# A decoder trunk kernel: another order of the steps where one sub-layer hands over to the next, and products sorted by kind

## Chip, cores and metric

One core of a Trainium2 chip runs the whole program in one launch. The metric is the device time of one execution in microseconds (us), median of several runs.

## What is computed

One decoder layer on 544 tokens (512 of a prompt, 8 x 4 of samples), width 1024:

```
rms(x, g) = x * rsqrt(mean(x*x) + 1e-6) * g
x = x + 0.5 * rms(ffn(rms(x, ffn1_pre_g)), ffn1_post_g)      # ffn(h) = (silu(h Wg) * (h Wu)) Wd, width 2816
x = x + rms(mix(rms(x, mix_pre_g)), mix_post_g)              # mix: one input projection (2432 columns), four
x = x + 0.5 * rms(ffn(rms(x, ffn2_pre_g)), ffn2_post_g)      # token mixers of width 256, one output projection
```

The mixers are a gated conv of width 3, a conv of width 31 with LayerNorm, RWKV-7 time mixing in four heads, and pooled means; their states are returned too. All is float32.

## The kernel before

The activations lie transposed: x is 8 rows (k or j, 128 features each) of 544 tokens; the tokens are halved into half 0 and half 1 of 272, since a PSUM bank takes 512 numbers. A *unit* is one tile of 128 output features. A weight tile comes by DMA into `raw` (2 slots, SP's queue), ScalarE copies it to `wh` (fp32r, `split_hi`, L284), VectorE takes the rest to `wl` (`split_lo`, L289); both have 4 slots. The input is split in the same way (`xh`, `xl`, or `hh`, `hl`). `product` forms for each row j and each half the three products wh x right_h, wh x right_l and wl x right_h (L305 to L307), accumulated in one bank per half. Unit s writes banks 2s and 2s+1 (`pair(s)`). Every engine has its own order written out by hand; semaphores join them, and VectorE and ScalarE take their steps strictly as written.

The program is FFN 1, a hand-over (n = 1), the mixer, a hand-over (n = 3), FFN 2, and an end (n = 5). In a hand-over the norm behind a sub-layer (gain g_n) and the one ahead of the next (g_n+1) are taken together:

- `last_units_pe`: of the last 8 output units, units 4 to 7 are made first for half 0, then for half 1 (`second`). VectorE takes each half out of PSUM (`leave_half`, L896 or L1967), forms its product with x (`half_cross_dve`, L472), ScalarE the squares (L466, L468), and VectorE adds the three sums of squares into `a3` (`half_squares_dve`, L488; of unit 7 in two steps, L491 and L494; of whole units `squares_dve`, L447).
- `half_sums_pe(n, h, second)` (L367) sums a3 over the partitions: first the squares of f, then (second) those of f*g and f*g*x, out of which the sum of squares of the new x follows, so that the next norm's root is known before x is. `var_dve` (L401), `half_root_act` (L386, L389; second L383), `half_rec_dve` (L409) and for the second `square_dve` (L418 to L426) make the factors, `half_spread_pe` (L376) spreads one over the partitions, `half_rb_act` (L393) copies it to SBUF.
- `rows_dve`: for each row k, update (L511: f*g*factor), add to x (L516), and `low` (L526, xl); ScalarE's `high_act` (L521) makes xh from the new x between add and low.
- `ramp_pe`: the first four units of the next sub-layer, made row by row as the rows come, half 0, then half 1. Unit 3 of half 0 joins at row 4 with five rows at once. At the end of half 1 the units finish one after the other.

Each of sums and spreads needs what VectorE has added; VectorE's `var_dve` and `square_dve` need the sums; `update` needs the copied factor; the row needs xl. Behind the ramp, VectorE takes the first unit out of PSUM (L1831 in the mixer) and the next unit's weight tile is split.

Of the kernel before, what the change touches and what calls it, by code (L numbers as in the profile page):

```python
# [32 lines left out]
KD = D // P  # L33
# [3 lines left out]
H = N // 2  # L37
# [77 lines left out]
def program(nc, a, o):  # L115

    with ExitStack() as ctx:
# [180 lines left out]
        def product(pe, out, s, order, right_h, right_l, before=None, opens=True, closes=True, parts=(0, 1)):  # L298

            for j in order:  # L300
                if before:
                    before(j)
                for n in parts:
                    col = slice(n * H, n * H + H)
                    pe.matmul(out[:, n], wh[:, s, j], right_h[:, j, col], start=opens and j == order[0], stop=False)  # L305
                    pe.matmul(out[:, n], wh[:, s, j], right_l[:, j, col], start=False, stop=False)  # L306
                    last = pe.matmul(out[:, n], wl[:, s, j], right_h[:, j, col], start=False, stop=closes and j == order[-1])  # L307
            return last


# [218 lines left out]
        def rows_dve(dve, n, h, first, last):  # L529

            for k in range(first, last):
                update_dve(dve, n, h, k)
                if k:
                    low_dve(dve, n, h, k - 1)
                add_dve(dve, n, h, k)
            if last == KD:
                low_dve(dve, n, h, KD - 1)

        def last_units_pe(pe, n, u0, first, order, right_h, right_l, free):

            for d in range(4, KD):
                split_ready(pe, u0, 0, first + d)
                free(d)
                product(pe, pair(d - 4), d - 4, order, right_h, right_l, parts=(0,)).then_inc(S("half_done"), 1)

            def second(d, lo, hi):
                return product(pe, pair(d - 4), d - 4, order[lo:hi], right_h, right_l, opens=lo == 0, closes=hi == KD, parts=(1,))

            second(4, 0, 5)
            half_sums_pe(pe, n, 0, 0)  # L550
            second(4, 5, 8).then_inc(S("unit_done"), 1)
            if n < 5:
                half_sums_pe(pe, n, 0, 1)
            second(5, 0, 2)
            half_spread_pe(pe, n, 0, 0)
            second(5, 2, 8).then_inc(S("unit_done"), 1)
            second(6, 0, 8).then_inc(S("unit_done"), 1)
            if n < 5:
                half_spread_pe(pe, n, 0, 1)
            second(7, 0, 8).then_inc(S("unit_done"), 1)  # L560

        def ramp_pe(pe, n, u):

            def come(h, j):
                pe.wait_ge(S("n_xl"), row(n, h, j) + 1)

            pe.wait_ge(S("n_rb"), mark(n, 0, 1) + 1)
            for j in range(KD):
                come(0, j)
                for s in range(3):  # L570
                    if j == 0:
                        split_ready(pe, u, 0, s)
                    product(pe, pair(s), s, (j,), xh, xl, opens=j == 0, closes=j == KD - 1, parts=(0,))
                if j == 2:
                    half_sums_pe(pe, n, 1, 0)
                if j == 3:
                    half_sums_pe(pe, n, 1, 1)
                    half_spread_pe(pe, n, 1, 0)
                if j == 4:
                    split_ready(pe, u, 0, 3)  # L580
                    product(pe, pair(3), 3, range(5), xh, xl, closes=False, parts=(0,))
                if j > 4:
                    product(pe, pair(3), 3, (j,), xh, xl, opens=False, closes=j == KD - 1, parts=(0,))
                if j == 5:
                    half_spread_pe(pe, n, 1, 1)
            pe.wait_ge(S("n_rb"), mark(n, 1, 1) + 1)
            for j in range(KD - 2):
                come(1, j)
                for s in range(4):
                    product(pe, pair(s), s, (j,), xh, xl, opens=j == 0, closes=False, parts=(1,))  # L590
            for s in range(4):
                product(pe, pair(s), s, (KD - 2, KD - 1), xh, xl, None if s else lambda j: come(1, j), opens=False, parts=(1,)
                        ).then_inc(S("unit_done"), 1)

        def hand_over_act(act, n, u):
            for d in range(4, KD):
                half_squares_act(act, n, 0, d)
            half_root_act(act, n, 0, 0)
            split_hi(act, u, 0, 0, KD)
            half_squares_act(act, n, 1, 4)  # L600
            half_rb_act(act, n, 0, 0)
            high_act(act, n, 0, 0)
            split_hi(act, u, 0, 1, KD)
            half_root_act(act, n, 0, 1)
            high_act(act, n, 0, 1)
            half_squares_act(act, n, 1, 5)
            split_hi(act, u, 0, 2, KD)
            half_rb_act(act, n, 0, 1)
            high_act(act, n, 0, 2)
            half_squares_act(act, n, 1, 6)  # L610
            high_act(act, n, 0, 3)
            split_hi(act, u, 0, 3, KD)
            half_squares_act(act, n, 1, 7)
            half_root_act(act, n, 1, 0)
            high_act(act, n, 0, 4)
            high_act(act, n, 0, 5)
            half_rb_act(act, n, 1, 0)
            high_act(act, n, 0, 6)
            half_root_act(act, n, 1, 1)
            high_act(act, n, 0, 7)  # L620
            high_act(act, n, 1, 0)
            half_rb_act(act, n, 1, 1)
            for k in range(1, KD):
                high_act(act, n, 1, k)

        def hand_over_dve(dve, n, u, leave_half):
            for d in range(4, KD):
                leave_half(0, d)
                half_cross_dve(dve, n, 0, d)
                half_squares_dve(dve, n, 0, d)  # L630
            var_dve(dve, n, 0)
            half_rec_dve(dve, n, 0, 0)
            leave_half(1, 4)
            half_cross_dve(dve, n, 1, 4)
            split_lo(dve, u, 0, 0, KD)
            half_squares_dve(dve, n, 1, 4)
            rows_dve(dve, n, 0, 0, 1)
            square_dve(dve, n, 0)
            rows_dve(dve, n, 0, 1, 2)
            leave_half(1, 5)  # L640
            half_cross_dve(dve, n, 1, 5)
            half_rec_dve(dve, n, 0, 1)
            split_lo(dve, u, 0, 1, KD)
            rows_dve(dve, n, 0, 2, 3)
            half_squares_dve(dve, n, 1, 5)
            split_lo(dve, u, 0, 2, KD)
            leave_half(1, 6)
            half_cross_dve(dve, n, 1, 6)
            rows_dve(dve, n, 0, 3, 4)
            leave_half(1, 7)  # L650
            half_cross_dve(dve, n, 1, 7)
            half_squares_dve(dve, n, 1, 6)
            half_squares_dve(dve, n, 1, 7)
            var_dve(dve, n, 1)
            rows_dve(dve, n, 0, 4, 5)
            half_rec_dve(dve, n, 1, 0)
            split_lo(dve, u, 0, 3, KD)
            rows_dve(dve, n, 0, 5, 6)
            square_dve(dve, n, 1)
            rows_dve(dve, n, 0, 6, 7)  # L660
            half_rec_dve(dve, n, 1, 1)
            rows_dve(dve, n, 0, 7, 8)
            rows_dve(dve, n, 1, 0, 8)

        BY_POOL = (0, 1, 3, 4, 6)

# [160 lines left out]
        def ffn_act(act, q, u0, n):  # L827
            u = u0
# [3 lines left out]
            for g, (f0, nf) in enumerate(GROUPS):  # L832
# [11 lines left out]
                            silu_act(act, q, i, f0, 1 + s // 2)  # L844
                u += 2 * nf
                for s in range(KD):
                    if g == 2 and s == 7:
                        down_act(act, q, g, 3, n)
                    split_hi(act, u, 0, s, nf)
                    if s == 1:  # L850
                        silu_act(act, q, 0, f0, nf - 1)
                        if g == 2:
                            act.activation(st2[:, 1, 6:7], ones[:, 0:1], ACT.Sqrt)
                    if g == 2 and 2 <= s < 5:
                        down_act(act, q, g, s - 2, n)
                u += KD

        def ffn_dve(dve, q, u0, n):
# [4 lines left out]
            for g, (f0, nf) in enumerate(GROUPS):  # L863
# [20 lines left out]
                    if g == 2 and s == 6:  # L884
                        down_dve(dve, q, u, g, 3, n)
                u += KD
            squares_dve(dve, n, 3)

            def leave_half(h, d):
                if h:  # L890
# [788 lines left out]
        def mixer_act(act):  # L1679
# [64 lines left out]
                act.wait_ge(S("c_y"), p + 1)  # L1744
                split_y_hi(act, 6 + p)
            for m in range(4):
                if m == 2:
                    split_hi(act, MIX0, 0, OUT0 + 4 + m, KD)
                act.wait_ge(S("o_out"), m + 1)
                squares_act(act, 3, m, f[:, m], par_("g3", m))  # L1750
                if m != 2:
                    split_hi(act, MIX0, 0, OUT0 + 4 + m, KD)

        def mixer_dve(dve):
# [194 lines left out]
            for m in range(4):  # L1949
# [7 lines left out]
                cross_dve(dve, 3, m)  # L1957
                if m != 2:
                    split_lo(dve, MIX0, 0, OUT0 + 4 + m, KD)
            squares_dve(dve, 3, 3)  # L1960

            def leave_half(h, d):
                if h:
# [161 lines left out]
```

## Time and profile before

| | |
|---|---|
| median of 3 runs | 1209.89 us (1205.71 to 1211.03) |
| the profiled execution | 1210.43 us, span of its instructions 1208.6 us |
| busy: TensorE, its weight loads | 1151.0 us (95%), 1128.4 us (93%) |
| busy: VectorE, ScalarE, GpSimd | 626.6 us (52%), 336.8 us (28%), 40.2 us (3%) |
| DMA | 92.23 MB, 76 GB/s over the span |
| first hand-over, second hand-over | about 396 to 457, 754 to 815 us of the span |

All times in the rows are us from the span's start. Busy times are shares of the span per engine and overlap each other. A matmul's record lasts longer than the distance to the next one, since matmuls are pipelined; the distance between two starts is what one costs.

### The profile page before, as it was taken

What the parts mean: (1) busy time and instruction counts of PE and PEld (TensorE: products, weight loads), DVE (VectorE), ACT (ScalarE), POOL (GpSimd) and SP (SyncE); (2) the same over time, 40 slices, a digit from 0 to 9 for tenths busy, and PEclk for the clock granted to TensorE, in tenths of its full rate; (3) what the DMA queues carried; (4) which work ended last, traced back from release to release, by engine and by line L of the source; (5) the groups of instructions that cost most, each with busy time, mean ns of one, the idle gap of its engine ahead of it and who ended that gap; (6) DMA issues with size and microseconds to landing.
All of it is one profiled execution on the core that took longest, in us unless ns stands there. A gap on an engine that the chain in (4) does not pass through costs nothing.

```text
span 1208.6 us, 21735 instructions
## 1 busy us (share of the span) xinstructions
PE 1151.0 (95%) x8994; PEld 1128.4 (93%) x8994; DVE 626.6 (52%) x1075; ACT 336.8 (28%) x496; POOL 40.2 (3%) x57
## 2 busy tenths in 40 slices
PE   6999999999999997999898989999999999999996
PEld 6999999999999997998777889899999999999996
DVE  5533343333345775889767526865333343334346
ACT  5321222112223433521234343433122221122220
POOL 0000000000000000210221100000000000000001
PEclk9999999999999888999899989889999999999998
DMA  6313232223232211332500002203233232323222
GB/s 229 105 53 104 89 102 71 88 87 103 71 102 78 65 50 53 76 88 76 41 10 28 1 1 73 70 18 105 69 106 102 72 103 72 105 70 101 72 70 75
DMA packets 35391, 92.23 MB, mean 76 GB/s; under 512 B 10368, under 2 KB 12928, under 8 KB 35200
## 3 DMA queue, kind: packets, MB, share of 16 engines
q1 hardware_dynamic: 33744, 87.67, 24.5%
q10 hardware_dynamic: 1584, 3.68, 0.8%
q8 instruction: 45, 0.74, 0.3%
q14 instruction: 18, 0.15, 0.0%
HBM read 88.05 MB, written 3.28 MB: 76 GB/s over the span
## 4 chain that ended last, share of the span: by engine, by line
PE 83%; DVE 11%; issue 3%; ACT 2%; DMA 1%; ACTq 0%; DVEq 0%; SPq 0%
PE ps L305 24%; PE ps L307 24%; PE ps L306 24%; PE ps L1131 1%; DVE wl L289 1%; PE ps L1137 1%; PE ps L1138 1%; PE ps L367 1%; DVE mixf L984 1%; ACT wh L284 1%; DVE a L447 1%; PE ps L376 1%; DVE tb L676 1%; PE ps L1573 1%; DVE xx L1310 0%
## 5 line engine op out<-in xcount | busy, mean ns | idle before, releaser
L305 PE MATMUL ps<-xh,wh 128*128 128x272 f32 x1840 | 543.1, 295 | 24.9 <-DVE xl L503 11.0
L307 PE MATMUL ps<-xh,wl 128*128 128x272 f32 x1840 | 538.5, 293 | 0.0
L306 PE MATMUL ps<-xl,wh 128*128 128x272 f32 x1840 | 535.9, 291 | 0.0
L305 PEld LDWEIGHTS ps<-xh,wh 128*128 128x128 f32 x1840 | 352.9, 192 | 27.4 <-DVE wl L289 17.4
L306 PEld LDWEIGHTS ps<-xl,wh 128*128 128x128 f32 x1840 | 353.6, 192 | 0.1
L307 PEld LDWEIGHTS ps<-xh,wl 128*128 128x128 f32 x1840 | 352.4, 192 | 0.0
L284 ACT ACTIVATE wh<-raw 128x1024 fp32r<-128x1024 f32 (+1 forms) x163 | 167.8, 1033 | 322.1 <-PE ps L307 199.4
L289 DVE TENSOR_TENSOR wl<-raw,wh 128x1024 fp32r<-128x1024 f32 (+1 forms) x163 | 192.5, 1202 | 46.3 <-ACT wh L284 46.0
L305 PE MATMUL ps<-hh,wh 128*128 128x272 f32 x704 | 204.1, 290 | 0.0
L307 PE MATMUL ps<-hh,wl 128*128 128x272 f32 x704 | 203.6, 289 | 0.0
L306 PE MATMUL ps<-hl,wh 128*128 128x272 f32 x704 | 203.0, 288 | 0.0
L797 DVE TENSOR_TENSOR h<-silu,ps 128x544 f32<-128x544 f32 x44 | 31.7, 721 | 212.6 <-PE ps L307 210.6
L306 PEld LDWEIGHTS ps<-hl,wh 128*128 128x128 f32 x704 | 133.4, 190 | 0.0
L305 PEld LDWEIGHTS ps<-hh,wh 128*128 128x128 f32 x704 | 133.2, 189 | 0.0
L307 PEld LDWEIGHTS ps<-hh,wl 128*128 128x128 f32 x704 | 133.1, 189 | 0.0
L783 ACT ACTIVATE silu<-silu 128x544 f32<-128x544 f32 x44 | 29.0, 659 | 233.9 <-DVE silu L793 233.9
L793 DVE TENSOR_TENSOR silu<-ps,rb 128x544 f32<-128x544 f32 x44 | 31.8, 724 | 80.2 <-PE ps L307 75.9
L816 DVE TENSOR_TENSOR f<-ps,f 128x544 f32<-128x544 f32 x24 | 17.4, 724 | 76.3 <-PE ps L307 76.3
L984 DVE SCALAR_TENSOR_TENSOR mixf<-zb,par,mixf 128x512 f32<-128x512 f32 x60 | 44.6, 743 | 0.1
L804 DVE TENSOR_TENSOR hl<-h,hh 128x544 f32 (+1 forms) x44 | 31.9, 725 | 4.3
L813 DVE COPY f<-ps 128x544 f32<-128x544 f32 x16 | 11.6, 724 | 43.2 <-PE ps L307 43.2
L1310 DVE TENSOR_TENSOR xx<-ps,con 128x256 f32<-128x256 f32 x40 | 16.7, 422 | 26.9 <-PE ps L1131 26.4
(311 smaller groups left out, 855.4 us busy)
## 6 DMA issues: line engine op xcount, KB each, us to landing
raw<-in_w_gu SPq DMA_DIRECT2D x88, 512.0 KB, 3.7
raw<-in_w_d SPq DMA_DIRECT2D x32, 512.0 KB, 3.7
raw<-in_w_in SPq DMA_DIRECT2D x19, 512.0 KB, 3.7
raw<-in_w_d SPq DMA_DIRECT2D x16, 384.0 KB, 3.1
raw<-in_w_out SPq DMA_DIRECT2D x8, 512.0 KB, 3.7
x<-in_x ACTq DMA_DIRECT2D x8, 272.0 KB, 6.8
out_y<-x SPq DMA_DIRECT2D x16, 136.0 KB, 1.8
con<-in_con ACTq DMA_DIRECT2D x1, 1158.5 KB, 9.3
```

Of the source, the lines that this page charges most:

```text
L284: act.activation(wh[:, s % 4, 0:k, :], raw[:, s % RAW, 0:k, :], ACT.Copy).then_inc(S("w_hi"), 1 + skip)
L289: dve.tensor_tensor(wl[:, s % 4, 0:k, :], raw[:, s % RAW, 0:k, :], wh[:, s % 4, 0:k, :].bitcast(F32), SUB).then_inc(S("w_lo"), 1 + skip)
L305: pe.matmul(out[:, n], wh[:, s, j], right_h[:, j, col], start=opens and j == order[0], stop=False)
L306: pe.matmul(out[:, n], wh[:, s, j], right_l[:, j, col], start=False, stop=False)
L307: last = pe.matmul(out[:, n], wl[:, s, j], right_h[:, j, col], start=False, stop=closes and j == order[-1])
L783: act.activation(silu[:, s % 2], silu[:, s % 2], ACT.Silu).then_inc(S(f"silu{q}"), 1)
L793: dve.tensor_tensor(halves(silu[:, s % 2]), pair(2 * (s % 2)), halves(rb[:]), MUL).then_inc(S(f"gate{q}"), 1)
L797: dve.tensor_tensor(halves(h32[:, s % 2]), halves(silu[:, s % 2]), pair(2 * (s % 2) + 1), MUL).then_inc(S(f"h_mul{q}"), 1)
L804: dve.tensor_tensor(hl[:, j].rearrange(one), h32[:, s % 2], hh[:, j].rearrange(one).bitcast(F32), SUB).then_inc(S(f"h_lo{q}"), 1)
L816: dve.tensor_tensor(halves(f[:, d]), pair(d % 4), halves(f[:, d]), ADD).then_inc(S(f"d_out{q}"), 1)
L984: eng.scalar_tensor_tensor(y1, z1, w, y1, MUL, ADD)
L1310: dve.tensor_tensor(xx[:, p], done(p)[:, 0:2 * P].rearrange(HC, h=2), C_("lev", k=l * P).unsqueeze(1).to_broadcast([P, 2, P]), MUL).then_i ...
```

## The change

The order of steps changes, and no work is added or removed. In `product` the three kinds are the outer loop and the two halves the inner one. In the hand-overs: the last whole unit's squares (`squares_dve`, 3) and each half unit's squares are added a unit later; TensorE's first sums stand after six rows of unit 4 and the second root's sums go from there to unit 6 (half 0), and from row 3 to behind the loop (half 1); the first sums of half 1 go from row 2 to row 4; the spreads move with them; waits for `h_square` are added ahead of unit 1 in the ramp, where its bank held those sums; unit 3 joins at row 4 in both halves; ScalarE's and VectorE's orders are rewritten to fit; in a row, the add stands right behind the update. In two places a weight copy of ScalarE goes ahead of a whole unit's squares.

```diff
@@ -300,11 +300,11 @@
             before(j)
-        for n in parts:
-            col = slice(n * H, n * H + H)
-            pe.matmul(out[:, n], wh[:, s, j], right_h[:, j, col], start=opens and j == order[0], stop=False)
-            pe.matmul(out[:, n], wh[:, s, j], right_l[:, j, col], start=False, stop=False)
-            last = pe.matmul(out[:, n], wl[:, s, j], right_h[:, j, col], start=False, stop=closes and j == order[-1])
+        for left, right in ((wh, right_h), (wh, right_l), (wl, right_h)):
+            first, final = left is wh and right is right_h, left is wl
+            for n in parts:
+                last = pe.matmul(out[:, n], left[:, s, j], right[:, j, n * H:n * H + H], start=first and opens and j == order[0],
+                                 stop=final and closes and j == order[-1])
     return last
@@ -530,9 +530,9 @@
         update_dve(dve, n, h, k)
+        add_dve(dve, n, h, k)
         if k:
             low_dve(dve, n, h, k - 1)
-        add_dve(dve, n, h, k)
     if last == KD:
@@ -546,17 +546,16 @@
     def second(d, lo, hi):
...
-    second(4, 0, 5)
+    second(4, 0, 6)
     half_sums_pe(pe, n, 0, 0)
-    second(4, 5, 8).then_inc(S("unit_done"), 1)
+    second(4, 6, 8).then_inc(S("unit_done"), 1)
+    second(5, 0, 3)
+    half_spread_pe(pe, n, 0, 0)
+    second(5, 3, 8).then_inc(S("unit_done"), 1)
+    second(6, 0, 4)
     if n < 5:
         half_sums_pe(pe, n, 0, 1)
-    second(5, 0, 2)
-    half_spread_pe(pe, n, 0, 0)
-    second(5, 2, 8).then_inc(S("unit_done"), 1)
-    second(6, 0, 8).then_inc(S("unit_done"), 1)
-    if n < 5:
-        half_spread_pe(pe, n, 0, 1)
+    second(6, 4, 8).then_inc(S("unit_done"), 1)
     second(7, 0, 8).then_inc(S("unit_done"), 1)
...
 def ramp_pe(pe, n, u):
@@ -564,30 +563,41 @@
     def come(h, j):
...
-    pe.wait_ge(S("n_rb"), mark(n, 0, 1) + 1)
+    def fourth(h, j):
+        if j == 4:
+            split_ready(pe, u, 0, 3)
+            pe.wait_ge(S("n_rb"), mark(n, h, 1) + 1)
+            product(pe, pair(3), 3, range(5), xh, xl, closes=False, parts=(h,))
+        if j > 4:
+            product(pe, pair(3), 3, (j,), xh, xl, opens=False, closes=j == KD - 1, parts=(h,))
+
+    pe.wait_ge(S("n_rb"), mark(n, 0, 0) + 1)
     for j in range(KD):
...
                 split_ready(pe, u, 0, s)
+                if s == 1:
+                    pe.wait_ge(S("h_square"), 10 * (n // 2) + 2)
             product(pe, pair(s), s, (j,), xh, xl, opens=j == 0, closes=j == KD - 1, parts=(0,))
-        if j == 2:
+        if j == 1:
+            half_spread_pe(pe, n, 0, 1)
+        fourth(0, j)
+        if j == 4:
             half_sums_pe(pe, n, 1, 0)
-        if j == 3:
-            half_sums_pe(pe, n, 1, 1)
+        if j == 6:
             half_spread_pe(pe, n, 1, 0)
-        if j == 4:
-            split_ready(pe, u, 0, 3)
-            product(pe, pair(3), 3, range(5), xh, xl, closes=False, parts=(0,))
-        if j > 4:
-            product(pe, pair(3), 3, (j,), xh, xl, opens=False, closes=j == KD - 1, parts=(0,))
-        if j == 5:
-            half_spread_pe(pe, n, 1, 1)
-    pe.wait_ge(S("n_rb"), mark(n, 1, 1) + 1)
+    half_sums_pe(pe, n, 1, 1)
+    pe.wait_ge(S("n_rb"), mark(n, 1, 0) + 1)
     for j in range(KD - 2):
         come(1, j)
-        for s in range(4):
+        for s in range(3):
+            if j == 0 and s == 1:
+                pe.wait_ge(S("h_square"), 10 * (n // 2) + 5 + 2)
             product(pe, pair(s), s, (j,), xh, xl, opens=j == 0, closes=False, parts=(1,))
+        if j == 2:
+            half_spread_pe(pe, n, 1, 1)
+        fourth(1, j)
     for s in range(4):
@@ -597,70 +607,80 @@
     split_hi(act, u, 0, 0, KD)
+    half_rb_act(act, n, 0, 0)
     half_squares_act(act, n, 1, 4)
-    half_rb_act(act, n, 0, 0)
     high_act(act, n, 0, 0)
     split_hi(act, u, 0, 1, KD)
-    half_root_act(act, n, 0, 1)
     high_act(act, n, 0, 1)
...
     split_hi(act, u, 0, 2, KD)
-    half_rb_act(act, n, 0, 1)
     high_act(act, n, 0, 2)
+    half_root_act(act, n, 0, 1)
     half_squares_act(act, n, 1, 6)
...
     split_hi(act, u, 0, 3, KD)
+    half_rb_act(act, n, 0, 1)
     half_squares_act(act, n, 1, 7)
+    high_act(act, n, 0, 4)
     half_root_act(act, n, 1, 0)
-    high_act(act, n, 0, 4)
     high_act(act, n, 0, 5)
+    high_act(act, n, 0, 6)
+    high_act(act, n, 0, 7)
     half_rb_act(act, n, 1, 0)
-    high_act(act, n, 0, 6)
+    high_act(act, n, 1, 0)
     half_root_act(act, n, 1, 1)
-    high_act(act, n, 0, 7)
-    high_act(act, n, 1, 0)
+    for k in range(1, 4):
+        high_act(act, n, 1, k)
     half_rb_act(act, n, 1, 1)
-    for k in range(1, KD):
+    for k in range(4, KD):
         high_act(act, n, 1, k)
...
 def hand_over_dve(dve, n, u, leave_half):
     for d in range(4, KD):
+        if d == 7:
+            half_squares_dve(dve, n, 0, 6)
         leave_half(0, d)
         half_cross_dve(dve, n, 0, d)
-        half_squares_dve(dve, n, 0, d)
+        if d == 4:
+            squares_dve(dve, n, 3)
+        elif d < 7:
+            half_squares_dve(dve, n, 0, d - 1)
+    half_squares_dve(dve, n, 0, 7)
     var_dve(dve, n, 0)
...
     half_cross_dve(dve, n, 1, 4)
+    rows_dve(dve, n, 0, 0, 1)
     split_lo(dve, u, 0, 0, KD)
+    rows_dve(dve, n, 0, 1, 2)
     half_squares_dve(dve, n, 1, 4)
-    rows_dve(dve, n, 0, 0, 1)
-    square_dve(dve, n, 0)
-    rows_dve(dve, n, 0, 1, 2)
     leave_half(1, 5)
     half_cross_dve(dve, n, 1, 5)
-    half_rec_dve(dve, n, 0, 1)
     split_lo(dve, u, 0, 1, KD)
     rows_dve(dve, n, 0, 2, 3)
-    half_squares_dve(dve, n, 1, 5)
+    square_dve(dve, n, 0)
     split_lo(dve, u, 0, 2, KD)
...
     half_cross_dve(dve, n, 1, 6)
+    half_rec_dve(dve, n, 0, 1)
     rows_dve(dve, n, 0, 3, 4)
+    half_squares_dve(dve, n, 1, 5)
     leave_half(1, 7)
     half_cross_dve(dve, n, 1, 7)
+    rows_dve(dve, n, 0, 4, 5)
     half_squares_dve(dve, n, 1, 6)
+    split_lo(dve, u, 0, 3, KD)
     half_squares_dve(dve, n, 1, 7)
+    rows_dve(dve, n, 0, 5, 6)
     var_dve(dve, n, 1)
-    rows_dve(dve, n, 0, 4, 5)
+    rows_dve(dve, n, 0, 6, 7)
     half_rec_dve(dve, n, 1, 0)
-    split_lo(dve, u, 0, 3, KD)
-    rows_dve(dve, n, 0, 5, 6)
+    rows_dve(dve, n, 0, 7, 8)
+    rows_dve(dve, n, 1, 0, 1)
     square_dve(dve, n, 1)
-    rows_dve(dve, n, 0, 6, 7)
+    rows_dve(dve, n, 1, 1, 2)
     half_rec_dve(dve, n, 1, 1)
-    rows_dve(dve, n, 0, 7, 8)
-    rows_dve(dve, n, 1, 0, 8)
+    rows_dve(dve, n, 1, 2, 8)
@@ -844,9 +864,9 @@
         for s in range(KD):
+            split_hi(act, u, 0, s, nf)
             if g == 2 and s == 7:
                 down_act(act, q, g, 3, n)
-            split_hi(act, u, 0, s, nf)
             if s == 1:
@@ -884,7 +904,8 @@
         u += KD
-    squares_dve(dve, n, 3)
+    if n == 5:
+        squares_dve(dve, n, 3)
     def leave_half(h, d):
@@ -1744,11 +1765,11 @@
     for m in range(4):
-        if m == 2:
+        if m >= 2:
             split_hi(act, MIX0, 0, OUT0 + 4 + m, KD)
...
         squares_act(act, 3, m, f[:, m], par_("g3", m))
-        if m != 2:
+        if m < 2:
             split_hi(act, MIX0, 0, OUT0 + 4 + m, KD)
...
 def mixer_dve(dve):
@@ -1957,7 +1978,6 @@
             split_lo(dve, MIX0, 0, OUT0 + 4 + m, KD)
-    squares_dve(dve, 3, 3)
     def leave_half(h, d):
...
```

## Rows read from the trace of the kernel before

**Rows 1.** the page: the chain that ended last, shares of the span

```profile
PE 83%; DVE 11%; issue 3%; ACT 2%; DMA 1%; ACTq 0%; DVEq 0%; SPq 0%
```

**Rows 2.** stretches: busy us (x instructions) by engine, granted clock, DMA

```profile
130.00:220.00 90.00, 90.00 (x716) 90.00 (x715) 34.92 (x43) 20.30 (x23) 0.00 (x0) 1.00 0.28 88
230.00:260.00 30.00, 30.00 (x241) 30.00 (x241) 9.28 (x10) 5.31 (x5) 0.00 (x0) 1.00 0.30 88
425.70:429.00 3.30, 1.93 (x16) 1.62 (x14) 2.89 (x7) 1.41 (x4) 0.00 (x0) 1.00 0.01 2
429.10:439.30 10.20, 10.20 (x46) 10.20 (x47) 6.60 (x20) 2.67 (x6) 0.00 (x0) 0.50 0.40 139
787.50:797.60 10.10, 10.10 (x47) 10.10 (x48) 6.56 (x21) 2.67 (x6) 0.00 (x0) 0.50 0.15 54
```

**Rows 3.** VectorE in order of time, start and duration in us

```profile
395.06 1.23 DVE L289 TENSOR_TENSOR wl<-raw,wh 128x1024 fp32r<-128x1024 f32 x1 [1.70 <-ACT wh L284]
396.21 1.85 DVE L447 TENSOR_TENSOR a<-a,sq 128x1632 f32<-128x1632 f32 x1
397.98 0.43 DVE L896 TENSOR_TENSOR f<-ps,f 128x272 f32<-128x272 f32 x1
398.44 0.50 DVE L472 SCALAR_TENSOR_TENSOR sq<-f,par,x 128x272 f32<-128x272 f32 x1
399.37 1.01 DVE L488 TENSOR_TENSOR a<-a,sq 128x816 f32<-128x816 f32 x1 [0.43 <-ACT sq L468]
400.30 0.43 DVE L896 TENSOR_TENSOR f<-ps,f 128x272 f32<-128x272 f32 x1
...
405.95 0.44 DVE L491 TENSOR_TENSOR a<-a,sq 128x272 f32<-128x272 f32 x1
406.31 0.72 DVE L494 TENSOR_TENSOR a<-a,sq 128x544 f32<-128x544 f32 x1
```

**Rows 4.** TensorE's sums (L367) and spreads (L376), full or half clock

```profile
406.45 0.83 PE L367 MATMUL ps<-con,a 128*128 128x1 f32 x6 [1.81 <-DVE a L491]
...
408.36 2.34 PE L367 MATMUL ps<-con,a 128*128 128x1 f32 x12
...
412.06 1.29 PE L376 MATMUL ps<-con,st 128*128 128x128 f32 x6
...
441.47 0.74 PE L376 MATMUL ps<-con,st 128*128 128x128 f32 x6
```

**Rows 5.** ScalarE's copies of the spread factors

```profile
413.39 0.40 ACT L393 ACTIVATE rbp<-ps 128x272 f32<-128x272 f32 x1 [2.71 <-PE ps L376]
...
442.24 0.40 ACT L393 ACTIVATE rb<-ps 128x272 f32<-128x272 f32 x1 [1.71 <-PE ps L376]
```

**Rows 6.** VectorE: rows as before, and what stands between them

```profile
413.82 0.50 DVE L511 SCALAR_TENSOR_TENSOR tb<-f,par,rbp 128x272 f32<-128x272 f32 x1 [1.69 <-ACT rbp L393]
414.36 0.44 DVE L516 TENSOR_TENSOR x<-x,tb 128x272 f32<-128x272 f32 x1
414.72 0.15 DVE L418 SCALAR_TENSOR_TENSOR st<-ps,st 128x3 f32<-128x3 f32 x1
...
415.57 0.49 DVE L511 SCALAR_TENSOR_TENSOR tb<-f,par,rbp 128x272 f32<-128x272 f32 x1
415.98 0.49 DVE L526 SCALAR_TENSOR_TENSOR xl<-x,par,xh 128x272 fp32r<-128x272 f32 x1
416.39 0.43 DVE L516 TENSOR_TENSOR x<-x,tb 128x272 f32<-128x272 f32 x1
```

**Rows 7.** groups by line: the weight loads of two neighbours with one weight

```profile
L306 PEld LDWEIGHTS ps<-xl,wh 128*128 128x128 f32 x1840 | 353.6, 192 | 0.1
L305 PEld LDWEIGHTS ps<-xh,wh 128*128 128x128 f32 x1840 | 352.9, 192 | 27.4 <-DVE wl L289 17.4 <-issue 4.5 <-DVE xl L1554 3.2
```

**Rows 8.** VectorE: the wait after a ramp, and the last half

```profile
455.20 1.61 DVE L1831 TENSOR_TENSOR pc<-ps,rb 128x272 f32<-128x272 f32 x6 [2.66 <-PE ps L307]
...
1196.22 0.43 DVE L896 TENSOR_TENSOR f<-ps,f 128x272 f32<-128x272 f32 x1
```

## The prediction

> **What bounds the kernel now.** I read the page's chain first. TensorE holds 83% of it, VectorE 11% [rows 1], so a saving must shorten TensorE's stream or take waits out of it. Then the stretches: in plain products TensorE is busy throughout, one 272-column product per about 126 ns (714 whole ones in 90.00 us; 239 in 30.00 us with hh as the right side, 125.5 ns) [rows 2]. 272 columns at 2.4 GHz would be 113.3 ns, so 12 to 13 ns per product are something else. Third, the stretches of the hand-overs: there TensorE waits, and after it has waited its granted clock is 0.50, which is 1.2 GHz of the two levels: 429.10 to 439.30, right behind a stretch with 16 products in 3.3 us, and 787.50 to 797.60 in the second hand-over [rows 2]. A product then takes 0.227 us (272 columns at 1.2 GHz; 46 records in 10.20 us with the sums between). Last, the order of time of VectorE and TensorE there.
>
> I count a hand-over up to X, the end of the ramp's first unit, because the next unit waits for a chain that starts there: VectorE's first step is at 455.20, released by TensorE [rows 8], so X = 454.9 now.
>
> **The change, part by part, first hand-over.**
>
> *Squares a unit later.* Now each of four units waits 0.43 us for ScalarE [rows 3]. In the new order VectorE leaves unit 4 at 396.21 instead of adding the last full squares (1.77), adds them behind its cross product, and then adds the squares of unit d-1. By the steps of [rows 3] (leave 0.46, cross 0.42, add 0.93): unit 5 left at 398.87, 6 at 400.69, add, 7 at 403.44; its squares need 1.0 us more, 404.44 in place of 405.95. The sums follow 0.5 us later, at 404.95 for 406.45 [rows 4]. TensorE now idles 1.81 us there; with three products more ahead of the sums (18 x 0.126 from 402.6) it arrives at 404.9 and idles no more. The 1.5 us alone is a gain.
>
> *Spread ahead of the second root's sums.* Now 12 sum matmuls (2.34 us) lie between, and the first spread takes 1.29 us at half clock; undisturbed it takes 0.74 [rows 4]. New: sums to 405.65, six products to 406.5, nine to 407.6, spread, ScalarE's copy 0.77 us behind the spread's start as at 441.47 and 442.24 [rows 4, 5] at 408.4, first update at 408.8 for 413.82 [rows 6]: 5.0 us earlier. VectorE leaves unit 4 of the second half at 406.7 in between and idles 1.2 us. TensorE goes on with 15 + 12 products, 12 sums (1.34 at full clock), 12 + 24 products, and enters the ramp at 417.6. (12 sums by the six in 0.83, whose last runs out after the others: 0.112 apart, an estimate.)
>
> *Add straight after update.* Now update, low of the row before, add cost 0.41 + 0.41 + 0.36 [rows 6]. Without the low between, the add starts 0.54 after its update, as at 413.82 and 414.36 [rows 6]: a row costs 1.31 for about 1.19. What comes back is that low no longer waits for ScalarE, where it does now.
>
> *The chain of rows.* From 408.8 VectorE has no wait until row 4's low: six rows, of which the first is update and add alone (0.9 + 5 x 1.31 = 7.45), four weight copies' low parts (4 x 1.15), three adds (2.8), the last pair (1.08), three leaves with cross (2.65), the square (0.85) and a reciprocal (0.1) [rows 3, 6]: 19.5 us, 428.3. ScalarE's parts hide beside it: each wh copy (about 1.05) follows the unit that frees its slot, at 408, 412, 416 and 422 at the latest, ahead of its low part; the copy of the second factor is wanted only at row 4. TensorE waits in the ramp for rows 2, 3 and 4, 5.6 us in all.
>
> *The wait that the change adds.* half_sums_pe(n, 1, 0) moves from behind row 2 to behind row 4 and the fourth unit's five catch-up products. VectorE's var_dve(n, 1) stands right behind row 4's low, so VectorE is held until TensorE has done 9 + 15 products and six sums: 3.0 + 0.87 us at full clock (six sums are 0.83 [rows 4], VectorE starts 0.04 behind), at least 3.9 us, and behind it are rows 5 to 7, for which TensorE waits in turn. On SP's queue the load of the states and two weight loads wait for the last of half 1's sums; these come at 441 at the earliest, 14 us ahead of X. Then in one line, full clock: var 432.3; low 5 at 433.8; 24 products to 436.9; spread, copy, update of half 1's row 0 at 438.1; 12 products and the 12 sums to 440.7; square 0.85; row 1's update at 441.5; row 4's low at 448.2; 24 + 12 + 6 products, X = 453.6. That is 1.3 us earlier than now: most of the 5.0 us is given back.
>
> *The clock on top.* Waiting 2.0 and 3.3 us around nine products (rows 3 and 4) looks like the 425.70 stretch, which half clock follows [rows 2]. The 24 products of row 4 would then take up to 5.4 us for 3.0; I take 1.9 more there, 0.9 for rows 5 and 6, 1.2 at half 1's start behind the last sums: 4.0 us between the bounds 0 and about 8 (all of it at 1.2 GHz). X = 457.6, 2.7 us later than now. The Trainium skill, "TensorE: Matmul & The Clock Gate", section "HAM oscillation — how this bites in real kernels", says that a wait between bursts throttles TensorE again so that the next burst starts cold; by that rule the full-clock sum would not occur, and the trace's 0.50 stretches agree.
>
> *Second hand-over.* The same order. Here ScalarE's weight copy goes ahead of its squares, which frees VectorE 1.5 us sooner, but the sums are then bound by TensorE's own products, so it is hidden. It comes out 0.6 better: +2.1. If that cover were gone it would cost at most the 1.5.
>
> *The end.* The last sums and the spread stand three products later, 0.38 us, and VectorE is gapless from there to the last half at 1196.22, with no wait in its row [rows 8]: +0.4. The moves of squares_dve for n = 5 change nothing.
>
> *Products by kind.* 6,672 products in whole units change order: four neighbours with wh, two with wl, output halves alternating. Each keeps its own weight load: now L305 and L306 use the same weight one after the other and have 1840 loads each, 192 ns [rows 7]. No row shows alternating order alone, so I take 0; between the 125.5 and 126.1 ns of the two operands [rows 2] lies 0.6 ns, thus bounds of -4 and +4 us. The Trainium skill, same page, "Step-by-step: what each phase is for", says a weight can be loaded once and used for many matmuls. A rival below gives what that would be.
>
> **Sum.** 2.7 + 2.1 + 0.4 + 0 = 5.2 us on the profiled execution's 1210.4 us; that lies 0.5 above the median, so 1215.
>
> **Rivals.** (a) The clock stays up: -1.3 - 1.9 + 0.4 = -2.8, 1207. For it: the first part (to 422) has TensorE nearly full. Against: 5.6 us of waiting. (b) Slower: half clock lasts through the second root's sums and into half 1. It decides if TensorE falls to 1.2 GHz again after row 5, so that update of row 1 comes past 447; +4 more per hand-over, 1222. (c) By kind shortens a product by 0.6 ns: 1211 with the waits, 1203 without. (d) The repeated loads fall away and with them the 12 ns above the columns: 6,672 x 12.6 ns = 84 us, 1126. Against it are the equal counts [rows 7]; this is what the page's load-once rule would mean here. (e) The reorder does what it says: VectorE is not held, because row 4 arrives earlier than I add up; then 5 us per hand-over stay, 1201. Against it: nineteen steps with measured durations.
>
> **Numbers.** Forecast 0.45 (own range 1211 to 1219), (a) 0.17, (b) 0.15, (c) 0.13, (d) 0.01, (e) 0.09. A measurement of this kernel tells about 0.5%, 6 us. Slower by that: 0.4 of the forecast's and all of (b), 0.33 with rounding down for its low end. Faster: (e), (d) and part of (c), 0.16. Range 1202 to 1222: what lies outside is (d), half of (e), and the far side of (b).
>
> **What would show it.** First update at 408.8 for 413.82, TensorE without idle ahead of the first sums (right: the squares). An idle of 4 to 6 us ahead of var at L401 in half 1, released by the sums. Granted clock 0.50 within the ramps. The add 0.53 behind its update. Mean time of a product in plain units 126 ns again, and 1840 loads per group. The prediction is wrong if var does not wait, or if plain units change by over 0.3 ns.

## The result, and the profile after

The changed kernel takes 1216.18 us (median of 20 runs, 1211.67 to 1218.90), the kernel before 1210.44 (20 runs, 1202.81 to 1218.01): ratio 1.0044, 95% interval 1.0027 to 1.0062, 5.3 us slower. I had forecast 1215 and +5.2. The size is right, but two terms in it were wrong and cancelled, as the experiments show; that the sum came out is luck. The profiled execution took 1216.28 us, span 1214.5.

The chain of the page after, to lay beside [rows 1]:

```profile
PE 85%; DVE 11%; issue 2%; ACT 1%; ACTq 0%; DVEq 0%
```

Stretches after: two of plain products (to lay beside [rows 2]), then the first hand-over from the first half product of unit 4 to VectorE's first step behind the ramp, the mixer up to the second hand-over, and that hand-over:

```profile
130.00:220.00 90.00, 90.00 (x721) 90.00 (x720) 34.93 (x43) 20.29 (x23) 0.00 (x0) 1.00 0.26 87
230.00:260.00 30.00, 30.00 (x243) 30.00 (x242) 9.28 (x10) 5.31 (x5) 0.00 (x0) 1.00 0.28 89
388.57:456.07 67.50, 58.56 (x431) 57.54 (x430) 48.15 (x100) 24.74 (x48) 1.66 (x8) 0.92 0.18 61
456.07:752.30 296.23, 268.90 (x2123) 247.37 (x2123) 205.25 (x458) 100.65 (x180) 35.63 (x40) 0.93 0.19 44
752.30:820.48 68.18, 59.52 (x430) 58.43 (x429) 48.22 (x101) 25.20 (x49) 0.00 (x0) 0.90 0.14 46
```

The same three stretches of the kernel before:

```profile
390.56:455.20 64.64, 61.46 (x431) 60.94 (x430) 47.82 (x101) 24.48 (x48) 1.53 (x8) 0.87 0.19 63
455.20:748.40 293.20, 267.29 (x2124) 246.35 (x2124) 204.75 (x458) 100.44 (x180) 34.80 (x40) 0.94 0.20 44
748.40:813.43 65.03, 61.36 (x429) 60.84 (x429) 47.90 (x101) 25.04 (x49) 0.00 (x0) 0.87 0.15 48
```

Three things are to be seen. In 90 us of plain products there are 721 instructions for 716, so a product is shorter. The hand-overs are 2.9 and 3.2 us longer. And within them TensorE's idle time (length less busy) rose from 3.2 and 3.7 us to 8.9 and 8.7, while its busy time fell by 2.9 and 1.8 because the granted clock is higher, 0.92 and 0.90 for 0.87.

Where the idle time lies, VectorE after, in order of time (beside [rows 3, 6]; the last line is the step behind the ramp, [rows 8]):

```profile
403.70 0.16 DVE L401 SCALAR_TENSOR_TENSOR st<-ps,st 128x3 f32<-128x3 f32 x1 [0.73 <-PE ps L367]
...
406.68 0.50 DVE L511 SCALAR_TENSOR_TENSOR tb<-f,par,rbp 128x272 f32<-128x272 f32 x1 [1.15 <-ACT rbp L393]
407.22 0.44 DVE L516 TENSOR_TENSOR x<-x,tb 128x272 f32<-128x272 f32 x1
...
431.39 0.16 DVE L401 SCALAR_TENSOR_TENSOR st<-ps,st 128x3 f32<-128x3 f32 x1 [5.36 <-PE ps L367]
...
438.68 0.50 DVE L511 SCALAR_TENSOR_TENSOR tb<-f,par,rbp 128x272 f32<-128x272 f32 x1 [3.79 <-ACT rbp L393]
...
456.07 1.20 DVE L1852 TENSOR_TENSOR pc<-ps,rb 128x272 f32<-128x272 f32 x4 [2.16 <-PE ps L306]
```

TensorE after: the ramp's waits for rows 3 and 4, then half 1's sums and spreads (beside [rows 4]), and the last spread of the kernel:

```profile
421.74 0.39 PE L306 MATMUL ps<-xh,wh 128*128 128x272 f32 x1 [1.71 <-DVE xl L526]
...
426.08 0.60 PE L306 MATMUL ps<-xh,wh 128*128 128x272 f32 x1 [2.94 <-DVE xl L526]
...
430.63 0.72 PE L367 MATMUL ps<-con,a 128*128 128x1 f32 x6
...
437.47 0.73 PE L376 MATMUL ps<-con,st 128*128 128x128 f32 x6
...
439.66 1.39 PE L367 MATMUL ps<-con,a 128*128 128x1 f32 x12
...
1204.49 1.46 PE L376 MATMUL ps<-con,st 128*128 128x128 f32 x6 [0.70 <-DVE st L409]
```

VectorE has row 4 done at 426.03 and then stands at L401 for 5.36 us until TensorE, which only then works through 24 products, has done the six sums. Half 1's first update waits again, for the spread. In the second hand-over the step at L401 has no record, and VectorE stands still for 5.83 us there, up to 796.55.

### The profile page after: what moved, and what is told of

The parts are those of the page before. It is cut to its first block, busy times and chain, and to the rows that moved or that the text cites. A ratio compares the mean times of both kernels' runs of the same rounds, so it can differ in the third digit from the quotient of the medians.

```text
span 1214.5 us, 21741 instructions
## 1 busy us (share of the span) xinstructions
PE 1143.7 (94%) x8994; PEld 1119.5 (92%) x8994; DVE 627.7 (52%) x1075; ACT 337.4 (28%) x496; POOL 41.2 (3%) x57
## 4 chain that ended last, share of the span: by engine, by line
PE 85%; DVE 11%; issue 2%; ACT 1%; ACTq 0%; DVEq 0%
PE ps L306 75%; DVE wl L289 1%; PE ps L1152 1%; DVE mixf L1005 1%; PE ps L1158 1%; PE ps L1159 1%; DVE xl L526 1%; DVE tb L696 1%; DVE tb L511 1%; DVE mixf L1006 1%; DVE xx L1331 1%; PE ps L367 1%; PE ps L1594 1%; PE ps L376 0%; DVE a L488 0%
## 5 line engine op out<-in xcount | busy, mean ns | idle before, releaser
L306 PE MATMUL ps<-xh,wh 128*128 128x272 f32 x1840 | 409.1, 295 | 41.5 <-DVE xl L526 17.4
L306 PE MATMUL ps<-xh,wl 128*128 128x272 f32 x1840 | 403.5, 292 | 0.0
L306 PE MATMUL ps<-xl,wh 128*128 128x272 f32 x1840 | 402.7, 292 | 0.0
L306 PEld LDWEIGHTS ps<-xh,wh 128*128 128x128 f32 x1840 | 303.2, 193 | 46.0 <-DVE wl L289 18.6
L306 PEld LDWEIGHTS ps<-xl,wh 128*128 128x128 f32 x1840 | 303.3, 193 | 0.0
L306 PEld LDWEIGHTS ps<-xh,wl 128*128 128x128 f32 x1840 | 301.0, 193 | 0.0
L306 PE MATMUL ps<-hh,wh 128*128 128x272 f32 x704 | 156.2, 288 | 0.0
L306 PE MATMUL ps<-hh,wl 128*128 128x272 f32 x704 | 155.4, 288 | 0.0
L306 PE MATMUL ps<-hl,wh 128*128 128x272 f32 x704 | 155.1, 287 | 0.0
L306 PEld LDWEIGHTS ps<-hh,wh 128*128 128x128 f32 x704 | 113.7, 188 | 0.0
```

The source lines that it names most:

```text
L306: last = pe.matmul(out[:, n], left[:, s, j], right[:, j, n * H:n * H + H], start=first and opens and j == order[0], stop=final and closes ...
```

## The experiments

Every ratio here is against runs of the kernel before on the same chip in the same job.

**1. Each half of the change alone.** `kind_only` is the kernel before with the new `product`, `order_only` the changed kernel with the old one.

```
# kind_only, against the kernel before     # order_only, against the changed kernel
- for n in parts:                          - for left, right in ((wh, right_h), ...):
-     three products of half n             -     for n in parts: one product
+ for left, right in ((wh, right_h), ...): + for n in parts:
+     for n in parts: one product          +     three products of half n
```

> The kernel before with the products by kind alone, every other step as before. Theory of the prediction: 0 us, a plain product stays at 126.1 ns. Theory from the changed trace (a plain product of xh went from 126.1 to 125.3 ns, one of hh from 125.3 to 124.4): 6,672 products x 0.87 ns = 5.8 us faster, ratio 0.995, and a plain unit of 48 products takes 6.01 us for 6.05. If only the total moved by chance (TensorE's clock stretches in the mixer), the ratio is 1.000 and the interval between products is 126.1 ns.

> The changed kernel with the products in the old order, thus the order of steps alone. The prediction's sum for the order is +5.2 us, ratio 1.004. If the products by kind gave 5.8 us back in the changed kernel, the order alone costs about 11 us, ratio 1.009; of it the two hand-overs hold 6 us (2.8 and 3.2, to the end of each ramp's first unit), the end 0.4 to 1, and what is left lies in the mixer.

Measured: products by kind alone 1206.2 us, ratio 0.9956 (0.993 to 0.9982), 5.3 us faster with an interval of 2.2 to 8.5; the reorder alone 1221.13 us, 1.0095 (1.0063 to 1.0126), 11.5 slower with an interval of 7.6 to 15.3. Each run also gives its span and granted clock. Span times clock is about what the execution would take at full clock. The half clock costs at most the remainder ("rest"), which also holds half-clock time in which TensorE waits anyway. As means of all runs (before: the 42 runs of the three jobs that the experiments ran in; the clocks of the 20 that the changed kernel was set against are not on record):

```
kernel       runs  span     span x clock  rest
before        42   1209.9   1169.8        40.1
kind_only     12   1204.4   1164.9        39.6
order_only     6   1219.9   1180.8        39.0
after         20   1214.2   1174.2        40.0
```

The reorder adds 11.0 us at full clock with the old products (`order_only` against before) and 9.3 with the new (after against `kind_only`). The remainder, 40 us, stays within about 1 us; single runs of one kernel spread in it by 1.6 to 3.4 us (standard deviation).

The two hand-overs of `order_only`:

```profile
390.64:458.66 68.02, 59.08 (x431) 58.01 (x430) 48.07 (x100) 24.73 (x48) 1.66 (x8) 0.90 0.18 60
758.09:826.45 68.36, 59.65 (x430) 58.59 (x429) 48.37 (x101) 25.36 (x50) 0.00 (x0) 0.90 0.15 46
```

TensorE idles 8.9 and 8.7 us in them, as in the changed kernel, and length times clock is 61.2 and 61.5 us for 56.2 and 56.6 in the kernel before. So at full clock the whole cost lies in the hand-overs, 5 us in each. As they ran they are 3.4 and 3.3 us longer than in the profile of before, near the 2.8 and 3.2 that I expected, because that profile holds more half clock.

**2. What in "by kind" shortens a product?** The new order changes three things between neighbours: they share a weight, they go to different output banks, and they read different halves of the right side. In `banks_apart` both alternate, but few neighbours share a weight. `banks_turn` alternates only the bank; `halves_turn` alternates the half of the right side and keeps the shared weights, but not the bank.

```
# pairs (kind, half); in the last two (kind, half, bank)
+ banks_apart: (wh h, 0) (wl h, 1) (wh l, 0) (wh h, 1) (wl h, 0) (wh l, 1)
+ banks_turn:  (wh h, 0, 0) (wh l, 0, 1) (wl h, 0, 0) (wh h, 1, 1) (wh l, 1, 0) (wl h, 1, 1)
+ halves_turn: (wh h, 0, 0) (wh h, 1, 0) (wh l, 0, 0) (wh l, 1, 1) (wl h, 0, 1) (wl h, 1, 1)
```

> The changed kernel with another order inside one row: wh.h0, wl.h1, wh.l0, wh.h1, wl.h0, wh.l1 - every neighbour writes the other bank, but only one neighbour of six loads the same weight (before: two, changed: four). If what shortens a product is that banks alternate, a plain unit keeps 125.3 ns (xh) and 124.4 ns (hh) per product; if it is that the same weight is loaded again, it is at 126.1 ns or above.

> Plain products in the old order of weights and right sides (half 0: wh xh, wh xl, wl xh; then half 1), but each goes to the other output bank than the one before it; the sums of the two halves get mixed, so the output is not the reference's. If it is the change of output bank between neighbours that gives the 0.87 ns, a plain product takes 125.3 ns (124.4 with hh); if it is the change of the right side's half, 126.1 (125.3).

> Plain products by kind with the halves of the right side in turn, but three neighbours in a row into each output bank; the sums of the two halves get mixed, so the output is not the reference's. If the change of output bank gives the 0.87 ns, a plain product takes 126.1 ns (125.3 with hh); if the right side's half, 125.3 (124.4).

The stretch 130 to 220 us of the three, `banks_apart` first, then `banks_turn`:

```profile
130.00:220.00 90.00, 90.00 (x721) 90.00 (x720) 34.89 (x43) 20.29 (x23) 0.00 (x0) 1.00 0.26 86
```

```profile
130.00:220.00 90.00, 90.00 (x716) 90.00 (x715) 34.93 (x43) 20.30 (x23) 0.00 (x0) 1.00 0.27 88
```

and `halves_turn`:

```profile
130.00:220.00 90.00, 90.00 (x721) 90.00 (x719) 34.73 (x44) 20.29 (x23) 0.00 (x0) 1.00 0.26 85
```

The distance between the starts of neighbours in a whole unit, as a mean, is 126.1 ns (125.3 with hh) in the kernel before, `order_only` and `banks_turn`, and 125.3 (124.4) in the changed kernel, `kind_only`, `banks_apart` and `halves_turn`; the difference is 0.83 ns in both stretches. What the four shorter ones have in common is that the right side's half changes at every neighbour. Neither the bank nor the weight shared by neighbours gives it.

It is a matter of the order as a whole and not of single pairs. In the kernel before (units between 130 and 220 us) the two neighbours of six that change the half are 127.2 and 125.1 ns apart, and the four that keep it 127.1, 128.0, 127.8 and 121.3, on average 126.2 and 126.1. Why alternating halves are shorter throughout, no run here shows. The whole kernels, one run each, took 1215.12 us (`banks_apart`), 1221.22 (`banks_turn`) and 1218.22 (`halves_turn`).

**3. Half 1's first sums earlier** (`sums_row3`):

```
- if j == 4: half_sums_pe(pe, n, 1, 0)     # behind fourth(0, j)
+ if j == 3: half_sums_pe(pe, n, 1, 0)     # ahead of fourth(0, j)
```

> The changed kernel with one step moved: the first sums of half 1 stand behind row 3 in the ramp instead of behind row 4 and the fourth unit's five products. Theory of the wait: VectorE's var step no longer waits 5.4 us; half 1's first update comes about 3.6 us sooner and each hand-over is 3.5 to 4 us shorter, 7 to 8 us in all, ratio to the kernel before 0.998. Rival (the clock, not the wait, is what costs): TensorE still waits for rows 3 and 4 and still falls to 1.2 GHz, the hand-overs shorten by under 1.5 us each, ratio 1.002 or more.

Measured 1210.26 us, ratio 0.9994 (0.9969 to 1.0019): 6 us of the changed kernel's time are gone. VectorE in this kernel:

```profile
424.59 0.15 DVE L401 SCALAR_TENSOR_TENSOR st<-ps,st 128x3 f32<-128x3 f32 x1
...
434.65 0.50 DVE L511 SCALAR_TENSOR_TENSOR tb<-f,par,rbp 128x272 f32<-128x272 f32 x1 [6.57 <-ACT rbp L393]
```

The wait at L401 is gone, and a longer one stands at half 1's first update: the root is ready at 425.96, but the spread stands behind row 6 in TensorE's order. The hand-overs are 65.2 and 64.8 us, thus 2.3 and 3.3 shorter than in the changed kernel's profile, where I gave 3.5 to 4. The named wait was a cause, and the next late hand-off took part of its place.

**4. All of half 1's sums and spreads earlier** (`all_early`):

```
+ if j == 4: half_sums_pe(pe, n, 1, 0); half_sums_pe(pe, n, 1, 1)   # ahead of row 4
+ if j == 4: half_spread_pe(pe, n, 1, 0)   # ahead of fourth(0, 4), was behind row 6
+ half_spread_pe(pe, n, 1, 1)              # behind half 0, was behind half 1's row 2
```

> The changed kernel with half 1's sums of both roots and its first spread moved ahead, behind rows 3 and 4 of the first half, and its second spread right behind the first half. Theory (the reorder is good and only the late sums and spreads of half 1 spoil it): VectorE has no wait at L401 and none of 6.6 us ahead of half 1's first update (as it had with the first sums alone behind row 3), TensorE has no 2.68 us idle behind the first half; hand-over about 61 us for 65.2 with the first sums moved alone and 67.5 in the changed kernel, whole kernel 1200 to 1204 us, ratio to before 0.992 to 0.995, below the products by kind alone (0.9956). Rival (VectorE's rows, 1.30 us each, set the end of the ramp whatever TensorE's order): 64 to 65 us, ratio 0.998 to 0.999. Rival by the clock: waits come elsewhere in the ramp, half clock stays 13.7 us per hand-over and takes 2 us back.

Measured 1201.97 us, ratio 0.9928 (0.9903 to 0.9954), hand-overs 63.2 and 62.2 us, a little more than I gave. TensorE's sums there start only at 425.19 and run at half clock, because they stand after the wait for row 4:

```profile
425.19 4.00 PE L367 MATMUL ps<-con,a 128*128 128x1 f32 x18 [2.94 <-DVE xl L526]
```

**5. The order in a row.** `rows_old` is the changed kernel with update, low, add again.

> The changed kernel with the old order in a row (update, low of the row before, add). By the prediction's prices (1.19 us a row in place of 1.31, but the low then waits for ScalarE in places) the hand-overs change by under 1 us: 66.5 to 68. By the trace of after (rows that set the pace follow at 1.30 us, in the kernel before at 1.44) they get longer: 68.5 to 69.5. Plain products 125.3 and 124.4 ns as in the changed kernel.

Hand-overs 66.5 and 67.2 us for 67.5 and 68.2 (the changed kernel profiled again: 66.3 and 68.0). The whole kernel took 1211.29 us in one run. In the second hand-over, where two executions of the changed kernel agree, the old order is 0.9 us shorter. My prices for rows hold (1.19 us for 1.31, six rows), and the expectation from the rows of half 1 fails: from half 1's first update to VectorE's step behind the ramp it takes 17.2 us in the second hand-over, for 17.5 in the changed kernel, so the old order is not the longer one there either. Most of the gain lies ahead of that update.

**6. Both, with the sums behind row 3.** `early_row3` is `all_early` with the 18 sum matmuls moved from after the wait for row 4 to behind row 3's products; `early_mixed` has in addition the old row order in half 0 and the new one in half 1.

```
+ if j == 3: half_sums_pe(pe, n, 1, 0); half_sums_pe(pe, n, 1, 1)
# early_mixed also, in rows_dve:
+ half 0: update, low(k - 1), add          half 1: update, add, low(k - 1)
```

> all_early with half 1's 18 sum matmuls behind row 3's products instead of after the wait for row 4 (in all_early they ran at half clock, 4.0 us from 425.19, and VectorE waited 1.53 us for the first six). Theory: they fill TensorE's wait for row 4, so VectorE's step at L401 does not wait and the hand-overs get 1 to 2 us shorter (61 to 62). Rival: the six sums of the first root go at the same time, but the second root's wait for VectorE's last squares keeps TensorE past row 4: no change.

> As all_early, with half 1's sums behind row 3's products instead of after the wait for row 4, and with the old order in a row (update, low, add) in half 0 and the new one in half 1. Theory (in half 0 VectorE has no wait for ScalarE, so the old order with 1.19 us a row is the better; in half 1 the rows follow one another alone, where the new one has 1.30 for 1.44): 0.7 to 1.0 us per hand-over from the rows and 0.5 to 1.5 from the sums, so hand-overs of 60.5 to 62 us (63.2 and 62.2 in all_early), whole kernel 1198 to 1201 us, ratio 0.990 to 0.992. Rival (TensorE alone sets the end of the ramp since half 1 is one run of 96 products): nothing beyond all_early's 0.9928.

Measured: `early_row3` 1201.09 us in one run, hand-overs 60.0 and 61.2. `early_mixed` 1197.38 us, ratio 0.9858 (0.9838 to 0.9879), 17 us faster than before: faster than both kernels and than the 1198 to 1201 that I expected. Its TensorE in the first hand-over:

```profile
423.51 2.35 PE L367 MATMUL ps<-con,a 128*128 128x1 f32 x18 [1.36 <-DVE a L491]
...
427.91 1.15 PE L376 MATMUL ps<-con,st 128*128 128x128 f32 x6
...
435.42 0.74 PE L376 MATMUL ps<-con,st 128*128 128x128 f32 x6
```

its VectorE behind the ramp:

```profile
446.15 1.20 DVE L1854 TENSOR_TENSOR pc<-ps,rb 128x272 f32<-128x272 f32 x4 [4.66 <-PE ps L306]
```

and its two hand-overs:

```profile
388.22:446.15 57.93, 55.38 (x431) 54.73 (x430) 47.42 (x100) 24.82 (x48) 1.66 (x8) 0.97 0.20 71
745.29:804.55 59.26, 56.66 (x430) 56.15 (x429) 47.55 (x100) 25.60 (x49) 0.00 (x0) 0.94 0.17 53
```

TensorE idles 2.6 us in each, and half 1 is one run of 96 products 126 ns apart, ahead of which VectorE has its rows ready. Here less half clock shows in the total as well: span times clock is 1163.1 (4 runs), 1.8 below `kind_only`, which is within what so few runs can tell, and the rest 32.0, against 40.7 for the 7 runs of before beside it. So most of what this version has over `kind_only` is half clock that does not occur. At full clock its hand-overs are no shorter than before: length times clock is 56.2 and 55.7 us, for 56.2 and 56.6. What the early sums do is to take TensorE's idle time away again (2.6 and 2.6 us for 8.9 and 8.7) and to keep TensorE's waits short: 1.36 us ahead of the sums at 423.51, where the changed kernel has 2.94 ahead of row 4, and the granted clock of the two hand-overs is 0.97 and 0.94 for 0.87. The new row order in half 1 was not tried without the rest.

**7. What belongs to an execution and what to the program.**

> The changed kernel unaltered. If the mixer's length and its half-clock time (296.2 us with 41.0 of it at half clock) belong to the program, they come again within 0.3 us; if they are the chance of an execution, they fall anywhere in what the other kernels with the new order showed, 293.7 to 299.4 with 37.5 to 44.4.

> The kernel before unaltered. If the mixer's length and its half-clock time (293.2 us with 34.1 of it at half clock) belong to the program, they come again within 0.3 us; if they are the chance of an execution, they fall anywhere in 293 to 299, and the 3 us that the change's trace had more in the mixer say nothing of the change.

The kernel before, profiled again (first hand-over, mixer, second hand-over):

```profile
389.70:451.19 61.49, 58.34 (x431) 57.81 (x430) 47.77 (x101) 24.37 (x48) 1.54 (x8) 0.92 0.20 67
451.19:750.84 299.65, 271.83 (x2124) 250.58 (x2124) 205.36 (x458) 100.41 (x180) 34.97 (x40) 0.93 0.18 44
750.84:815.99 65.15, 61.38 (x430) 60.86 (x429) 48.11 (x101) 25.14 (x50) 0.00 (x0) 0.87 0.14 47
```

The changed kernel, profiled again:

```profile
387.79:454.07 66.28, 57.33 (x431) 56.28 (x430) 48.14 (x101) 24.74 (x48) 1.66 (x8) 0.95 0.19 62
454.07:748.40 294.33, 266.37 (x2123) 244.92 (x2123) 205.49 (x458) 100.74 (x180) 34.90 (x40) 0.94 0.20 44
748.40:816.38 67.98, 59.28 (x430) 58.21 (x429) 48.26 (x100) 25.05 (x49) 0.00 (x0) 0.90 0.15 47
```

The mixer takes 293.2 and 299.7 us in one and the same program, 296.2 and 294.3 in the other; the 3 us that the first pair of traces showed there say nothing of the change. The two executions took 1211.55 us (before) and 1212.09 (changed). The first hand-over varies by 3.2 and 1.2 us, the second by 0.2. TensorE's idle time in it repeats: 3.2 and 3.2 us before, 8.9 and 9.0 after.

## Why the prediction was right in size and wrong in its terms

**Squares, spread, first update: right.** Counted from the first half product of unit 4, the sums were forecast at 14.4 us and came at 14.4, the first update at 18.2 and came at 18.1. TensorE no longer idles ahead of the sums. The add starts 0.54 behind its update.

**The wait that the change adds: right.** VectorE waits 5.36 us at L401, released by the sums (forecast 4 to 6). Half 1's first update came 50.1 us in (48.7 in the second profile), for a full-clock 47.5 and 2.8 of clock in the forecast. X was forecast 67.0 us in, and VectorE's step behind it came at 67.5. Experiment 3 shows the wait as a cause.

**The clock: mechanism right, its account wrong.** TensorE waits 1.71 and 2.94 us. Behind the first wait its products stay 0.13 us apart; behind the second, from 425.9 on, the granted clock is 0.50 and they are 0.23 apart. The Trainium skill, "TensorE: Matmul & The Clock Gate", section "HAM oscillation — how this bites in real kernels", says that the burst behind a gap starts cold; the trace agrees for the longer of the two waits. But I set the new hand-over against the profiled one of before, which held half-clock stretches of its own: a clock of 0.87 over 64.6 us, 8.4 us lost, where the other profile of it loses 4.9 (0.92 over 61.5). At full clock (length times clock, good to 0.3 us) the hand-overs grew from 56.2 and 56.6 us to 62.1 and 61.4, 5.9 and 4.8 longer, nearly all of it idle time; `order_only` gives 5.0 and 4.9. I credited the difference in half clock to the change. Over the whole kernel hardly any of it is left: the remainder is 40.1 us before and 40.0 after. So the step that failed is "1.3 us earlier than now" and with it "2.7 + 2.1": at full clock it should have been 5 to 6 and 5, and the reorder costs 9 to 11 us, as `order_only` measured, and not 5.2. Where the difference in half clock goes is open in part. The first pair of profiles has 10 us less of half-clock time in the changed kernel's hand-overs, the second pair 7, which is 3 to 5 us of loss; about 1 us of it goes at the end (10.3 us at half clock for 8.2), and the mixer varies by more than the rest from one execution of a program to the next.

**The end: +0.4 forecast, +1.05 found** (38.5 and 39.55 us from the last hand-over's start). `order_only` has 38.9, which is the 0.4. The rest is the last spread, which ran at half clock and took 1.46 us for 0.84. It takes 0.84 in the four profiles with the products' old spacing and 1.31 to 1.46 in all ten with the shorter one, `kind_only` among them, so it goes with the shorter products and not with the order of steps.

**Products by kind: this term failed.** "No row shows alternating order alone, so I take 0", with bounds of 4 us. It was 0.83 ns on 6,672 products, 5.5 us worked out and 5.3 measured, outside the bounds. They came from the difference between two operands, which has nothing to do with the order, and that difference was read too small: counting instructions in 90 and 30 us gave 0.6 ns, the starts give 126.1 and 125.3, thus 0.8. The text said that the prediction is wrong if plain units change by over 0.3 ns, and in this term it is. The loads did not fall away: 1840 for each kind, as in [rows 7]:

```profile
L306 PEld LDWEIGHTS ps<-xl,wh 128*128 128x128 f32 x1840 | 303.3, 193 | 0.0
L306 PEld LDWEIGHTS ps<-xh,wh 128*128 128x128 f32 x1840 | 303.2, 193 | 46.0 <-DVE wl L289 18.6 <-DVE xl L526 14.1 <-issue 9.5
```

**Rivals.** (a) did not happen. Of (b) the sign came, half clock again at row 5's products (432.9), but not the time: half 1's second update stands 53.4 us in, where (b) wanted over 56.4. (c) happened, with 0.83 ns for its 0.6; its 1211 came with hand-overs at 5.2, and with their true cost it is about the 1216 measured. (d) did not: the loads are as many as before. (e), the 5 us that stay, did not happen either. VectorE was held, and in `early_mixed`, which frees it, the hand-overs are 3.6 to 6.7 us shorter than in the two profiles of before, but by less half clock and not by a shorter chain: at full clock they are as long as before.

## What to carry to other kernels

When work of one engine is moved ahead, move with it what the other engines owe to the same chain: here half 1's sums and spreads, left late in TensorE's order, cost 9 to 11 us. With them in place the whole kernel is 16 to 17 us faster than before, of which about 5 are the products by kind and about 9 half clock that does not occur. Compare stretches by idle time and by time at full clock before crediting a stretch with its clock: idle time repeated to 0.1 us between executions, half-clock time did not. And where no row shows what an order of neighbours costs, the bound can't come from rows that differ in something else.

## What was not expected of the hardware

Products of 272 columns that change the half of the right side at every neighbour start 0.83 ns closer on average (125.3 for 126.1, 124.4 for 125.3 with hh) than in the order that changes it at every third, at full clock and with one weight load each; the output bank makes no difference of 0.05 ns. Within the old order the pairs that change the half are not the closer ones. The sums, 128 x 1 each, took 2.35 us for 18 in `early_mixed`, at a granted clock of 1.00 for all but the last of them, and 4.00 us for 18 in `all_early`, at 0.50; TensorE had waited 1.36 and 2.94 us just ahead.
